# Hybrid attention and recurrence block: gate_b units evicted raw with their sigmoids taken later, and adaLN accumulation steps moved within the attention passes

## What is computed

```python
mod = silu(c) @ w_ada + b_ada              # shift1, scale1, gate1, shift2, scale2, gate2
h = rms_norm(x, norm1_g) * (1 + scale1) + shift1
proj = h @ w_in                            # q_lat, a_k, a_v, k_idx, w_idx, b_q, b_f, b_i, b_g, gate_a, gate_b
out_a = dsa_attention(...)                 # 8 heads of 64, each query keeps 128 keys chosen by an indexer
out_b = rms_norm(hgrn2(...)) * silu(b_g)   # gated linear recurrence, 4 heads of 128
merged = sigmoid(gate_a) * (out_a @ w_proj_a) + sigmoid(gate_b) * (out_b @ w_proj_b)
x = x + gate1 * (merged @ w_out)
h2 = rms_norm(x, norm2_g) * (1 + scale2) + shift2
x = x + gate2 * (square(relu(h2 @ w_mlp1 + b_mlp1)) @ w_mlp2 + b_mlp2)
```

## Time and profile before

| | |
|---|---|
| median of three runs | 888.29 us |
| the profiled execution's own time | 887.42 us |
| its span, first to last instruction | 885.7 us |
| TensorE busy in the span | 836.6 us, 94% |
| VectorE busy | 461.0 us, 52% |
| ScalarE busy | 332.8 us, 38% |
| GpSimd busy | 222.1 us, 25% |
| DMA, all queues | 95.75 MB, mean 108 GB/s |

### The profile page before, as it was taken

One profiled execution on the slowest core, in us unless ns is written; L12 is line 12 of the kernel. 1 busy time (PEld: TensorE's weight loads), 2 busy tenths in 40 slices (PEclk: granted clock), 3 DMA queues, 4 the chain that ended last, 5 costly groups with the idle time before them and its releaser, 6 DMA issues.

```text
span 885.7 us, 10922 instructions
## 1 busy us (share of the span) xinstructions
PE 836.6 (94%) x3951; PEld 673.2 (76%) x3951; DVE 461.0 (52%) x713; ACT 332.8 (38%) x501; POOL 222.1 (25%) x127
## 2 busy tenths in 40 slices
PE   2699899989999999899899989999999999999998
PEld 1567668867878887666688878888888888888886
DVE  3932569995798786574585766952111122220000
ACT  2643434334343326566233234444111144442111
POOL 4023324430000000000000114544444444444440
PEclk9789989999999999899999989999999999999999
DMA  9922312331122222443355732833333333333303
GB/s 357 288 57 73 95 47 72 95 95 48 48 72 55 65 72 73 142 135 103 118 168 163 221 91 70 238 96 95 95 95 95 95 95 95 95 95 115 98 1 95
DMA packets 144554, 95.75 MB, mean 108 GB/s; under 512 B 8198, under 2 KB 138628, under 8 KB 143492
## 3 DMA queue, kind: packets, MB, share of 16 engines
q1 hardware_dynamic: 143104, 95.18, 36.3%
q10 hardware_dynamic: 1412, 0.07, 0.1%
HBM read 93.13 MB, written 2.10 MB: 108 GB/s over the span
## 4 chain that ended last, share of the span: by engine, by line
PE 80%; DVE 13%; ACT 3%; DMA 2%; issue 1%; ACTq 1%; SPq 0%; DVEq 0%
PE bank L1255 16%; PE bank L1256 16%; PE bank L1257 16%; PE bank L1405 3%; PE bank L1407 3%; PE bank L1406 3%; DVE score L967 3%; DVE top L965 2%; PE bank L1425 2%; PE bank L1597 2%; PE bank L1599 2%; PE bank L1598 2%; PE bank L1283 2%; DVE rt_k L927 1%; PE bank L1379 1%
## 5 line engine op out<-in xcount | busy, mean ns | idle before, releaser
L433 POOL TENSOR_TENSOR w_lo<-w_raw,w_hi 128x1024 fp32r<-128x1024 f32 x82 | 203.4, 2482 | 322.6 <-ACT w_hi L504 322.6
L1255 PE MATMUL bank<-h_hi,w_hi 128*128 128x512 f32 x464 | 184.8, 398 | 5.6 <-DVE h_lo L905 5.1
L504 ACT ACTIVATE w_hi<-w_raw 128x1024 fp32r<-128x1024 f32 x126 | 132.5, 1052 | 144.9 <-PE bank L1257 121.4
L1256 PE MATMUL bank<-h_lo,w_hi 128*128 128x512 f32 x464 | 182.5, 393 | 0.0
L1257 PE MATMUL bank<-h_hi,w_lo 128*128 128x512 f32 x464 | 182.5, 393 | 0.0
L1255 PEld LDWEIGHTS bank<-h_hi,w_hi 128*128 128x128 f32 x464 | 88.2, 190 | 29.9 <-issue 8.0
L1257 PEld LDWEIGHTS bank<-h_hi,w_lo 128*128 128x128 f32 x464 | 88.2, 190 | 18.8
L1256 PEld LDWEIGHTS bank<-h_lo,w_hi 128*128 128x128 f32 x464 | 88.3, 190 | 17.9 <-issue 0.2
L1255 PE MATMUL bank<-u_hi,w_hi 128*128 128x512 f32 x256 | 100.0, 391 | 0.0
L1257 PE MATMUL bank<-u_hi,w_lo 128*128 128x512 f32 x256 | 99.7, 389 | 0.0
L1256 PE MATMUL bank<-u_lo,w_hi 128*128 128x512 f32 x256 | 99.6, 389 | 0.0
(11 more groups left out here) (233 smaller groups left out, 1233.3 us busy)
## 6 DMA issues: line engine op xcount, KB each, us to landing
w_raw<-in_w_mlp SPq DMA_DIRECT2D x128, 256.0 KB, 3.0
w_raw<-in_w_in SPq DMA_DIRECT2D x88, 256.0 KB, 3.3
ada_raw<-in_w_ada SPq DMA_DIRECT2D x8, 1024.0 KB, 8.9
ada_even<-in_w_ada SPq DMA_DIRECT2D x16, 512.0 KB, 4.8
ada_odd<-in_w_ada SPq DMA_DIRECT2D x16, 512.0 KB, 4.9
w_raw<-in_w_out SPq DMA_DIRECT2D x16, 256.0 KB, 3.2
x_nat<-in_x SPq DMA_DIRECT2D x4, 512.0 KB, 5.9
w_raw<-in_w_proj_a SPq DMA_DIRECT2D x8, 256.0 KB, 2.9
```

Of the source, the lines that this page charges most:

```text
L433: nc.gpsimd.tensor_tensor(w_lo[:, s], w_raw[:, s], w_hi[:, s].bitcast(F32), ALU.subtract).then_inc(lo_ready, 1)
L504: nc.scalar.activation(w_hi[:, s], w_raw[:, s], ACT.Copy).then_inc(hi_ready, 1)
L1255: mm(bank[b][:], w_hi[:, slot, j], rhs_hi(i), start=f, stop=False)
L1256: mm(bank[b][:], w_hi[:, slot, j], rhs_lo(i), start=False, stop=False)
```

## The change

The eight gate_b units are evicted with a Copy in place of a Sigmoid, into the same tile sig_b. Their sigmoids are taken later, in place, from SBUF (new function gate_sigmoid, new semaphore sigb_ready): those of tiles 0 and 1 at the end of pass 3, after the last gate_b eviction and ahead of oa_head(2); that of tile m+2 in projection tile m, behind its split_hi. VectorE waits for sigb_ready before it multiplies with sig_b. The adaLN steps of a pass move on VectorE from ahead of its masks to the end of the pass. In SyncE's queue the order of the loads is the same as before; only the way it is written has changed.

```diff
-        ADA_PAIR = [0, 0, 3, 6, 8, 11]
+        ADA_PAIR = [0, 0, 3, 6, 8]
...
-            for p in range(1, PAIRS + 1):
+            for p in range(1, PAIRS):
                 load_proj(2 * p - 2)
                 load_proj(2 * p - 1)
                 for i in range(ADA_PAIR[p] + 2, ADA_PAIR[p + 1] + 2):
                     load_ada(i)
+            load_proj(KC - 2)
+            load_proj(KC - 1)
+            for i in range(KC + 2, KC + 5):
+                load_ada(i)
...
-                nc.scalar.activation(dst, bank[b][:], ACT.Sigmoid).then_inc(lin_evac, 1)
+                nc.scalar.activation(dst, bank[b][:], ACT.Copy).then_inc(lin_evac, 1)
                 split_hi(n + WS)
+
+            def gate_sigmoid(m):
+
+                act.wait_ge(lin_evac, G[U_M + KC + m + 1])
+                nc.scalar.activation(sig_b[:, m], sig_b[:, m], ACT.Sigmoid).then_inc(sigb_ready, 1)
...
                     gate(KC + 2 * p + 1, sig_b[:, 2 * p + 1])
+                    if p == PAIRS - 1:
+                        gate_sigmoid(0)
+                        gate_sigmoid(1)
                 if p:
                     oa_head(p - 1)
...
                 split_hi(n + WS)
+                if m + 2 < KC:
+                    gate_sigmoid(m + 2)
                 act.wait_ge(sum_ready, m + 1)
                 nc.scalar.activation(h_hi[:, m], sig_a[:, m], ACT.Copy).then_inc(mh_ready, 1)
...
                 if p < PAIRS:
-                    for i in range(ADA_PAIR[p], ADA_PAIR[p + 1]):
-                        ada_add(i)
                     if p:
                         dve.wait_ge(prob_turned, 8 * p)
...
                         head_out(BH - 1)
                         head_out_lo(BH - 1)
+                    for i in range(ADA_PAIR[p], ADA_PAIR[p + 1]):
+                        ada_add(i)
...
                 v.tensor_tensor(sa, bank[b][:], sa, ALU.mult)
+                dve.wait_ge(sigb_ready, m + 1)
                 step(v.tensor_tensor(sb, bank[b + 1][:], sb, ALU.mult))
```

More of the change, by code:

```diff
@@ L236, in hybrid_block @@
             sem("sqo_ready"), sem("sqo_added"), sem("orow_summed"), sem("orow_ready"), sem("orow_spread"))
+        sigb_ready = sem("sigb_ready")
         sum_ready, mh_ready, merged_ready = sem("sum_ready"), sem("mh_ready"), sem("merged_ready")
```

## The result

The changed kernel takes 880.78 us, the median of seven runs (879.03 to 883.44), beside 887.58 us for the kernel before in seven runs. The ratio is 0.9938, interval 0.992 to 0.9956, so about 5.5 us less (3.9 to 7.1); the two medians lie 6.80 us apart. Measured twice more, on other occasions, the ratio was 0.9940 (0.9921 to 0.9958) and 0.9947 (0.9929 to 0.9965). The forecast was 881.4 us and 6.88 us less. The median of the first seven lies where it was forecast, but three ratios of 0.9938 to 0.9947 say 4.7 to 5.5 us less, so the sum was somewhat too large. The profiles show where.

The account below looks back on a forecast made before the run. TensorE, busy for 94% of the span, was taken to bound the kernel. The table load's 1.28 and the steps' 5.60 us sum to 6.88, so 888.29 - 6.88 = 881.4 us, range 879.0 to 885.0.

Parts of the forecast that it names:

- The steps: In TensorE's first turn, moving the adaLN steps saves 5.60 us: 3.14 of stall on masks and 2.46 of low clock.
- The spare time: On VectorE between passes, masks of passes 2 and 3 would be ready 2.5 us (0.8) ahead of need, costing nothing.
- Rivals 2 and 3: Masks late in pass 2 or 3: one pass, 882.4 to 886.9 us, chance 0.12; both passes, 892.6 us, chance 0.03.
- The table load: Ahead of TensorE's first turn, dropping the load between pass 0's Exps and the eviction saves 1.28 us, leaving 0.4 of stall.
- Rival 5: In ScalarE's evictions, a table switch costs more than its load, 1.38 us more saved: 880.0 us, chance 0.03.
- Rival 4: Stall in pass 1 stays because something other than the steps holds the masks; only 1.28 us saved, 887.0, chance 0.03.
- rival 1: In the first turn the stall goes but the clock stays low; saved 1.28 + 3.14 us, time 883.9, chance 0.07.
- The sigmoids: On ScalarE in pass 3 and projection tiles 0 to 5, the later sigmoids fit into idle time and cost nothing.
- The clock behind the passes: Slow stretch of 1.76 us in tile 2 left in the forecast; range reaches 1.76 down and about as much up.

Follow-up runs that it names:

- e1: The changed kernel with the adaLN steps back ahead of the masks, so only the Copy evictions and later sigmoids remain; ratio to the kernel before 1.0006.
- before_again: The kernel before, unedited, profiled a second time; no run time given, 13.09 us from the logits of pass 0 to the first turn.
- e6: The kernel before with two dense gate_b blocks put between the logits of pass 0; ratio to the kernel before 1.0002, median 885.70 us.
- e2: The changed kernel with Sigmoid back in the evictions and no gate_sigmoid or its waits, so only the adaLN steps moved; ratio to the kernel before 0.9952.
- e3: The kernel before, adaLN steps still ahead of the masks, their numbers per pass changed from 0, 3, 3, 2 to 0, 2, 3, 3; ratio 0.9952.
- e8: The changed kernel with eight more VectorE instructions behind the adaLN steps of passes 1 and 2; ratio to the kernel before 0.9976.
- after_again: The changed kernel, unedited, measured and profiled once more; ratio to the kernel before 0.9940.
- e5: The changed kernel with two dense gate_b blocks put between the logits of pass 0; ratio to the kernel before 0.9904, median 878.52 us, four runs.
- e7: The changed kernel with the last recurrence head's sums ahead of the logits of pass 0 and two dense blocks between these; ratio to the kernel before 0.9919.
- e9: The kernel of e5 measured again, against the kernel before; ratio 0.9926.
- e10: The kernel of e7 measured again, against the kernel before; ratio 0.9912, median 878.12 us.
- after_third: The changed kernel, unedited, measured a third time; ratio to the kernel before 0.9947, median 882.04 us.

## Why the prediction came out, and the term that was too large

- **The steps, 5.60 us.** Right. From the first turn to values(0) before, e1, before_again and e6 took 23.22, 23.29, 23.78 and 22.57 us, the changed kernel 17.80, 17.80 and 17.60, so 4.8 to 6.2 us, and 5.42 in the first pair. The stall went from 3.39 to 0.25 and the low clock behind it with it. One reading on the way was wrong: the last transpositions of pass 0 do not end at 356.5 us, they start at 357.27, right ahead of the logits. Nothing hung on it, since the masks wait for the logits: in the changed kernel they start 1.27 us behind the first logits, as reckoned, after 4.09 us of idle time. e1 and e2 show that this term comes from the steps alone, e3 that within them it comes from the wait for block 2.
- **The spare time, 0.8 to 2.5 us.** VectorE had 3.81 and 3.73. The waits for the blocks were 2.58 and 2.14 us against the 3.1 that I took, and the work of the interval was 379.44 - 366.76 - 2.58 - 3.81 = 6.3 us against my 7.0. Rivals 2 and 3 had no ground; e8 shows the price they would have had: 1.96 and 1.26 us of stall for 2.0 and 1.3 of lateness, as reckoned, but the low clock behind one stall in two only.
- **The table load, 1.28 us.** This is the step that failed: "The next cover is TensorE's own work, which ended 1.68 us before that start, so 0.4 us of stall stays." That cover was read from one execution, in which the clock held in pass 0. It mostly does not, and then TensorE's work ends 1.6 us later and the term is 0.2. The mechanism was right where ScalarE is last (1.42 and 1.43 us measured). That stall of 1.68 us bounded the term, but did not say that a slower TensorE would take the place.
- **Rival 5** (2.66 us for a switch) is ruled out by 1.43. **Rival 4** and **rival 1** are ruled out by the stall of 0.25 and the clock of 1.00 in the first turn.
- **The sigmoids, nothing.** Right: 613 ns each, ScalarE idle 0.47 us ahead of the copy in tile 2, where it was 0.99. From values(0) to values(3), with two of the sigmoids, the times are 53.67 and 53.82 us, and the rest, with the other six, took 458.62 in after_again where it was 458.78 before.
- **The clock behind the passes.** I had left it unchanged and put it into the range. It came out between 0.3 us less and 1.4 more, mostly more.

With 0.2 for the load, where the clock falls, and 5.6 for the steps the sum is 5.8. With the 0.7 given back, which is not shown, it is 5.1, in the middle of what the three ratios say (4.7, 5.3 and 5.5 us). Their intervals reach from 3.1 to 7.1 us and do not tell 5.1 from 5.8. That the median came within 0.6 us of the forecast is in part luck: one term was 1.1 us too large in most executions.

## What to carry to other kernels

A stall that one execution shows bounds what its releaser is worth, apart from a low clock that may follow it (the 3.39 us of pass 1 were worth 5.4 to 5.6 with it); ask also how late the waiting engine itself can be, above all where its clock may be low in one execution and full in the next, and take a second profile before a term of 1 us is booked. When an in-order engine waits for a transfer that its own earlier step triggers, the cheapest cure is to see that the step and its transfer are not in the same stretch: here two numbers in a list were worth as much as moving the work. Idle time on the bottleneck engine can hide inside a busy row, when a run of small instructions takes longer than its parts.

## What was not expected of the hardware

The granted clock fell in pass 0 in seven of nine profiles of kernels with one order of work there. In e5, e6, e7, e9 and e10, with dense blocks between the sparse logits, it held five times in five; e7 and e10 also have the sums ahead of the logits. The Trainium skill (TensorE: Matmul & The Clock Gate, What's actually happening) says that the monitor runs freely, without a restart at the kernel's begin; the same program with and without the fall (before and before_again, changed and after_third) agrees with that. That a fall needs no stall of a microsecond was new to me: between the first logits and the one in pass 0 TensorE showed 0.14 us of idle time, inside the row of the logits, which themselves waited for masks, and then single-column sums.
